# One-column sums moved behind other products, sums copied ahead of tile copies, and the bias table written in eight masked parts

## What is computed

```python
# first block
sh1, sc1, g1, sh2, sc2, g2 = split(silu(c) @ ada_w + ada_b, 6)
h = rms_norm(x) * (1 + sc1) + sh1
x = x + g1 * rms_norm(hybrid_mixer(h))        # 8 heads of attention beside 8 groups of convolution
h = rms_norm(x) * (1 + sc2) + sh2
x = x + g2 * rms_norm(swiglu_ffn(h))
# second block
sh1, sc1, g1, sh2, sc2, g2 = split(silu(c_2) @ w_ada_2 + b_ada_2, 6)
h  = modulate(rms_norm(x), sh1, sc1)
hc = modulate(rms_norm(ctx_2), csh1, csc1)
x = x + g1 * neighbourhood_attention(h, hc)   # scores get a bias from na_rpb_2 and a column mask
x = x + g2 * conv_ffn(modulate(rms_norm(x), sh2, sc2))
```

## Time and profile before

| | us |
|---|---|
| median of 3 runs | 2663.33 (2661.33 to 2666.87) |
| the profiled execution, its own time | 2672.45 |
| its span, first to last instruction | 2670.7 |
| TensorE busy | 2594.7 (97%) |
| VectorE busy | 1839.3 (69%) |
| ScalarE busy | 1301.4 (49%) |
| GpSimd busy | 138.0 (5%) |
| mean share of full TensorE clock granted | 0.986 |

### The profile page before, as it was taken

One profiled execution on the slowest core, in us unless ns is written; L12 is line 12 of the kernel. 1 busy time (PEld: TensorE's weight loads), 2 busy tenths in 40 slices (PEclk: granted clock), 3 DMA queues, 4 the chain that ended last, 5 costly groups with the idle time before them and its releaser, 6 DMA issues.

```text
span 2670.7 us, 38186 instructions
## 1 busy us (share of the span) xinstructions
PE 2594.7 (97%) x13356; PEld 2138.9 (80%) x13356; DVE 1839.3 (69%) x2280; ACT 1301.4 (49%) x1856; POOL 138.0 (5%) x237
## 2 busy tenths in 40 slices
PE   7999899899999999999999999999999999999999
PEld 4677777787788888888787878787888888888887
DVE  2349778777888696888765556555578876667565
ACT  2349655444344344465625242424465556565544
POOL 3112011000200000000001000100000000000000
PEclk8999999899999999999999999999999999999999
DMA  9989777589888687789454545554568866666565
GB/s 352 377 292 370 208 284 247 191 299 335 274 292 284 215 286 254 250 297 324 138 192 142 189 137 177 158 178 142 166 212 283 284 190 190 189 178 203 192 194 167
DMA packets 236447, 622.97 MB, mean 233 GB/s; under 512 B 20172, under 2 KB 24567, under 8 KB 231408
## 3 DMA queue, kind: packets, MB, share of 16 engines
q1 hardware_dynamic: 213392, 525.40, 59.6%
q0 software_dynamic: 22144, 91.84, 10.2%
q10 hardware_dynamic: 800, 4.25, 0.4%
HBM read 613.80 MB, written 7.60 MB: 233 GB/s over the span
## 4 chain that ended last, share of the span: by engine, by line
PE 78%; DMA 10%; DVE 6%; issue 3%; ACT 3%; SPq 0%; DVEq 0%; ACTq 0%; POOL 0%
PE ps L2292 11%; PE ps L2233 11%; PE ps L2237 11%; PE ps L2235 10%; PE ps L2294 6%; PE ps L2687 6%; PE ps L2689 6%; PE ps L2691 6%; DMA raw<-in_w_in 2%; DMA slot<-in_ada_w 2%; DVE w_lo L1393 2%; DMA raw<-in_w_down 2%; DMA ada<-in_ada_w 2%; PE ps L2269 2%; PE ps L2273 1%
## 5 line engine op out<-in xcount | busy, mean ns | idle before, releaser
L1393 DVE TENSOR_TENSOR w_lo<-raw,w_hi 128x1024 fp32r<-128x1024 f32 x762 | 927.2, 1223 | 596.7 <-ACT w_hi L756 594.6
L756 ACT ACTIVATE w_hi<-raw 128x1024 fp32r<-128x1024 f32 x762 | 804.8, 1058 | 1000.3 <-PE ps L2237 406.8
L2292 PE MATMUL ps<-h_both,w_hi 128*128 128x512 f32 (+1 forms) x1392 | 480.7, 392 | 2.7 <-DVE h_both L1471 1.7
L2233 PE MATMUL ps<-w_hi,h_both 128*128 128x512 f32 x1152 | 467.3, 406 | 8.1 <-DVE w_lo L1393 4.8
L2237 PE MATMUL ps<-w_hi,h_both 128*128 128x512 f32 x1152 | 453.4, 394 | 0.0
L2235 PE MATMUL ps<-w_lo,h_both 128*128 128x512 f32 x1152 | 453.0, 393 | 0.0
L2294 PE MATMUL ps<-h_both,w_lo 128*128 128x256 f32 (+1 forms) x1392 | 386.6, 278 | 0.0
L2292 PEld LDWEIGHTS ps<-h_both,w_hi 128*128 128x128 f32 x1392 | 261.2, 188 | 60.9 <-DVE h_both L1471 2.4
L1405 DVE SCALAR_TENSOR_TENSOR acc<-ada,cact,acc 128x1024 f32<-128x1024 f32 x224 | 291.8, 1303 | 8.5 <-DMA ada<-in_w_ada 5.6
L2687 PE MATMUL ps<-w_hi,f_hi 128*128 128x512 f32 x680 | 266.6, 392 | 3.2 <-DVE f_lo L1664 1.8
L2233 PEld LDWEIGHTS ps<-w_hi,h_both 128*128 128x128 f32 x1152 | 218.2, 189 | 60.5 <-DVE w_lo L1393 8.3
(11 more groups left out here) (282 smaller groups left out, 3196.8 us busy)
## 6 DMA issues: line engine op xcount, KB each, us to landing
ada<-in_w_ada SPq DMA_DIRECT2D x192, 512.0 KB, 4.3
raw<-in_ffn_w_up SPq DMA_DIRECT2D x160, 512.0 KB, 4.5
slot<-in_ada_w POOLq DMA_DIRECT2D x60, 1024.0 KB, 9.0
raw<-in_na_w_qkv SPq DMA_DIRECT2D x96, 512.0 KB, 4.8
raw<-in_w_gate SPq DMA_DIRECT2D x88, 512.0 KB, 5.1
raw<-in_w_up SPq DMA_DIRECT2D x88, 512.0 KB, 4.7
raw<-in_w_down SPq DMA_DIRECT2D x88, 512.0 KB, 5.4
raw<-in_ffn_w_down SPq DMA_DIRECT2D x86, 512.0 KB, 4.6
```

Of the source, the lines that this page charges most:

```text
L756: act.activation(w_hi[:, s, :], raw[:, s, :], ACT.Copy).then_inc(hi_ready, 1)
L1393: dve.tensor_tensor(w_lo[:, s, :], raw[:, s, :], w_hi[:, s, :].bitcast(F32), ALU.subtract).then_inc(lo_ready, 1)
L2233: pe.matmul(o, hi_[:, k, a], wh, start=(k == 0), stop=False)
L2292: pe.matmul(ps[:, 4 * part + g, :].rearrange("p (a n) -> p a n", a=2)[:, :, n], w_hi[:, s, a], h_both[:, :, k, n], start=(k == 0 and ts[-1 ...
```

## The change

The diff, cut to its core:

```diff
-        TABLE_DMAS = H2 + 2 * TABLE_PARTS + 1
+        TABLE_DMAS = H2 + 3 * TABLE_PARTS
+        TABLE_AFTER = (4, 18, 32, 46, 56, 62, 68, 74)
...
-            for n in range(TABLE_PARTS):
-                pool.wait_ge(tile_used, T_FF1 + RING + 4 + 7 * n)
+            for n, tile in enumerate(TABLE_AFTER):
+                pool.wait_ge(tile_used, T_FF1 + RING + tile)
+                rows = slice(n * TABLE_ROWS, (n + 1) * TABLE_ROWS)
...
-            v = skew_s[:, :, 0:GRID - W]
-            link(pool.affine_select(out=v, in_=v, compare_op=ALU.is_ge, fill=NEG, base=WH,
-                                    pattern=[[0, H2 * DR], [1, GRID - W]], channel_multiplier=-1))
...
-            pool.dma_start(skew_d, skew_s[:, :, :]).then_inc(table_landed, 16)
+                v = skew_s[:, rows, 0:GRID - W]
+                link(pool.affine_select(out=v, in_=v, compare_op=ALU.is_ge, fill=NEG, base=WH,
+                                        pattern=[[0, TABLE_ROWS], [1, GRID - W]], channel_multiplier=-1))
...
+                pool.dma_start(skew_d[:, rows, :], skew_s[:, rows, :]).then_inc(table_landed, 16)
# ACT, opening
                 if q:
-                    for n in range(6 * q, 6 * q + 3):
-                        hi(T_AG, n)
+                    hi(T_AG, 6 * q)
+                    hi(T_AG, 6 * q + 1)
                 evacuate_sums(2 * q + 1)
                 start_hi(q)
                 if q:
+                    hi(T_AG, 6 * q + 2)
                     hi(T_AG, 6 * q + 3)
# DVE, opening
                 shift_of(2 * q)
-                if q:
-                    lo(T_AG, 6 * q + 2)
                 scale_of(2 * q + 1)
                 start_lo(q)
                 if q:
+                    lo(T_AG, 6 * q + 2)
                     lo(T_AG, 6 * q + 3)
# ACT, between the blocks
+            def b_g1_rows(cs):
+                for c in cs:
+                    act.wait_ge(g1_sums, c + 1)
+                    act.activation(acc0[:, c * C:(c + 1) * C], ps[:, c, :], ACT.Copy).then_inc(g1_read, 1)
...
                     hi(Tend, j)
+                    if j in (5, 6):
+                        b_g1_rows((2 * j - 10, 2 * j - 9))
# DVE, between the blocks
-                after()
...
-            def b_g1_rows():
-                for c in range(4):
-                    dve.wait_ge(g1_sums, c + 1)
-                    dve.tensor_copy(acc0[:, c * C:(c + 1) * C], ps[:, c, :]).then_inc(g1_read, 1)
-                clear(acc1)
...
             for e in range(2, 4):
                 split_ctx(e)
+            dve.wait_ge(g1_sums, 4)
+            clear(acc1)
             dve.wait_ge(acc_bias[1], 64)
# DVE, out_turn
+                y_gated(phase, 0, 0, bufs[1])
                 scale()
-                y_gated(phase, 0, 0, bufs[1])
# PE
-            def column_sums(accs, units_, m_, bank=6):
+            def column_sums(accs, units_, m_, bank=6, after=0):
+                for _ in range(after):
+                    yield
...
-                                             between=between if j > 1 or t == 0 else iter(()))
+                                             between=iter(()) if t else between)
...
-            qkv2(2, 1, between=column_sums((acc1,), 10 * UNITS, M["b_sh2"]))
+            qkv2(2, 1, between=column_sums((acc1,), 10 * UNITS, M["b_sh2"], after=12))
```

More of the change, by code:

```diff
@@ L696, in _ @@
             pool.wait_ge(table_landed, 16 * (H2 + TABLE_PARTS))
-            for n in range(TABLE_PARTS):
-                pool.wait_ge(tile_used, T_FF1 + RING + 4 + 7 * n)
+            W, WH = 16, 8
+            for n, tile in enumerate(TABLE_AFTER):
+                pool.wait_ge(tile_used, T_FF1 + RING + tile)
+                rows = slice(n * TABLE_ROWS, (n + 1) * TABLE_ROWS)
                 src = bass.AP(table_d.tensor, n * TABLE_ROWS * GRID * LANES + GRID - 1,
                               [[LANES - 1, GRID], [GRID * LANES, TABLE_ROWS], [1, GRID]])
-                pool.dma_start(skew_s[:, n * TABLE_ROWS:(n + 1) * TABLE_ROWS, :], src).then_inc(table_landed, 16)
-                pool.wait_ge(table_landed, 16 * (H2 + TABLE_PARTS + n + 1))
-            W, WH = 16, 8
-            v = skew_s[:, :, 0:GRID - W]
-            link(pool.affine_select(out=v, in_=v, compare_op=ALU.is_ge, fill=NEG, base=WH,
-                                    pattern=[[0, H2 * DR], [1, GRID - W]], channel_multiplier=-1))
-            v = skew_s[:, :, W:GRID]
-            link(pool.affine_select(out=v, in_=v, compare_op=ALU.is_gt, fill=NEG, base=WH - W,
-                                    pattern=[[0, H2 * DR], [-1, GRID - W]], channel_multiplier=1))
-            pool.dma_start(skew_d, skew_s[:, :, :]).then_inc(table_landed, 16)
+                pool.dma_start(skew_s[:, rows, :], src).then_inc(table_landed, 16)
+                pool.wait_ge(table_landed, 16 * (H2 + TABLE_PARTS + 2 * n + 1))
+                v = skew_s[:, rows, 0:GRID - W]
+                link(pool.affine_select(out=v, in_=v, compare_op=ALU.is_ge, fill=NEG, base=WH,
+                                        pattern=[[0, TABLE_ROWS], [1, GRID - W]], channel_multiplier=-1))
+                v = skew_s[:, rows, W:GRID]
+                link(pool.affine_select(out=v, in_=v, compare_op=ALU.is_gt, fill=NEG, base=WH - W,
+                                        pattern=[[0, TABLE_ROWS], [-1, GRID - W]], channel_multiplier=1))
+                pool.dma_start(skew_d[:, rows, :], skew_s[:, rows, :]).then_inc(table_landed, 16)
             pool.wait_ge(table_landed, 16 * TABLE_DMAS)
@@ L1803, in out_turn, with down_turn @@
                     lo(Tend, j)
-            def down_turn(n, phase, Tend, bufs, n0, m_, after, beside):
+            def down_turn(n, phase, Tend, bufs, n0, m_, beside):
                 def rows(s_):
@@ L2027, in _ @@
                        True, PH_DOWN1, d_ctx)
-            def b_g1_rows():
-                for c in range(4):
-                    dve.wait_ge(g1_sums, c + 1)
-                    dve.tensor_copy(acc0[:, c * C:(c + 1) * C], ps[:, c, :]).then_inc(g1_read, 1)
-                clear(acc1)
-            down_turn(8, PH_DOWN1, T_QKV2, down_bufs, 18, M["lat"], b_g1_rows, split_ctx)
+            down_turn(8, PH_DOWN1, T_QKV2, down_bufs, 18, M["lat"], split_ctx)
             for e in range(2, 4):
                 split_ctx(e)
+            dve.wait_ge(g1_sums, 4)
+            clear(acc1)
             dve.wait_ge(acc_bias[1], 64)
```

## The result

The changed kernel took 2642.66 us (median of 4 runs, 2637.05 to 2643.56), the kernel before 2662.33 in the same set (4 runs, 2660.57 to 2666.87): ratio 0.9919, 95% interval 0.9900 to 0.9938, 19.7 us less. The forecast was 2637.0 in a range of 2628 to 2652. Two later sets with 5 and 4 runs of the changed kernel gave 25.6 us less (2643.95 against 2669.52, ratio 0.9907, 0.9893 to 0.9922) and 24.5 less (2639.98 against 2664.47, 0.9904, 0.9879 to 0.9928).

The account below looks back on a forecast made before the run. TensorE, busy 2594.7 of 2670.7 us, was taken as the bound, so only its waits and half clock could be won. Terms 4.0 + 9.9 + 4.3 + 1.5 + 6.5 = 26.2 off the median 2663.33 gave 2637.0, range 2628 to 2652.

Parts of the forecast that it names:

- First output product: Sums at the first output product: moved behind the products of `t = 0`, they save wait and half clock, 9.9 us.
- Table: First feed-forward network: eight small masks and writes replace two large masks and one write, removing one TensorE stop, 4.3 us.
- Opening: Opening, fourth quarter: copy to `sums` ahead of ScalarE's third tile, removing TensorE's wait and lost clock, 4.0 us.
- Rival B: Only the sums pay; opening, table and copies between the blocks give nothing: 16.4 us saved, 2646.9; chance 0.14.
- Between the blocks: Between the blocks: ScalarE takes VectorE's four copies ahead of the splits of `ctx_2`, shortening TensorE's wait, 1.5 us.
- Third pass: Sums in the third pass: twelve bare products first (`after=12`) keep the clock full, 6.5 us, bounds 0 to 7.
- Rival A: The clock falls at the sums of first output product and third pass all the same: 11.7 us saved, 2651.6; chance 0.16.
- Rival C: First feed-forward network: each of the table's eight parts makes a stop like the single one, 8.2 us slower, 2671.5; chance 0.03.
- rival D: The change does more than listed: a second `w_lo` wait may go with its clock, 3 us more, 2634; chance 0.05.

Follow-up runs that it names:

- the kernel with `after=0`: Changed kernel with the third pass's sixteen sums directly behind the wait instead of behind twelve products (`after=12`); run twice: 2644.26 and 2638.61 us.

## Why the prediction was right, and where it was off

**First output product** (9.9): measured 8.3 by the medians of one set and 7.4 to 9.2 by profiles; within its bounds of 7 to 12. The mechanism held, including the wait for `w_lo` left at 490.4 and the clock. Of my 9.9, the wait is the smaller part: the profile of the run with the old wait and the new order loses 1.7.

**Table** (4.3): 4.8 by the medians and 4.3 by the profile. I had it all behind the write; in one of three profiles with the old table it came from the mask instead, by the wait of 3.47 us for `acc`. The price of a small mask was too low, mostly 1.2 to 2.3 us for 0.8 beside a working VectorE, and didn't matter.

**Opening** (4.0): 4.0 to 5.8 by 150 us. The fourth quarter gave it, the second little, as argued. Rival B, that the transfers take it back, has the profiles against it: all three with the old opening are 4.0 to 5.8 us later by 150 us, the ten others -2.2 to 0.6. The ratios point the same way. Its price is off too: of its 9.9 + 6.5 for the sums only 8.3 was there.

**Between the blocks** (1.5): 2.3 to 3.9 in profiles, because a short wait there can also drop the clock, which I had left out. The timed runs can't tell it from nothing.

**Third pass** (6.5): the step that failed. It measured 6.5 in one execution of four and nothing in three, and 0.3 and -1.4 in two timed comparisons. I had its bound of 0 for the case that the clock falls anyway after the change; what happened is that it mostly doesn't fall before it either. I should have seen the warning: 2672.45 for the profiled execution against a median of 2663.33 means 9.1 us that most executions don't lose. I read terms from an execution 9.1 us above the median and took them off the median.

Taking the terms as the times give them, 8.3 + 4.8 + (5 to 9) + (-1 to 3) + 0 = 17 to 25, against 19.7, 25.6 and 24.5 in the three sets. So 2637.0 was partly luck: with one of its five terms missing, the sum still comes near because the opening and the copies between the blocks may give more than forecast. That the first set falls 6.5 us short of 26.2, just the missing term, is a coincidence, since the other two sets reach 25.6 and 24.5 without it. Rival A is refuted where it was asked: in none of nine profiles with the new order of the first output product, nor in ten with that of the third pass, is the clock at half for most of the sums. Rival C, a stop for each part, is refuted by 0.3 us of waits for `w_lo` in that network, at most 1.5 in any profile with the new table. For rival D there is a coincidence only: the wait for `w_lo` near 645 us was absent from the second profile of before as well, and from that of the old table.

The rule of the Trainium skill that the prediction weighed ("TensorE: Matmul & The Clock Gate", section "What's actually happening": sustained activity lifts the slow state) can be placed now. Bare products behind a wait of 3.29 us brought the clock back, which agrees. Products alternating with one-column sums, busy for 5.00 of 5.00 us, did not for 13.7 to 17.1 us: busy time as the profile counts it was not enough there.

## What to carry to other kernels

Where TensorE has just been idle for some microseconds, put full products first and narrow ones (one-column sums) behind them: sixteen sums directly behind a wait of 3.4 us, wait included, cost 7 to 9 us here, and the same wait with bare products ahead of the sums 1.7. Behind a wait of 0.94 us the order was worth nothing in the median. Before a stretch at half clock is put down to the order of the code, look at a second profile of the same kernel, and hold the profiled execution's own time against the median: what is above it is bad luck of that one execution, and no change can take it off the median. A large transfer and a large mask that each can stop TensorE once are worth cutting; moving other transfers into a stretch that is already short of them was not.

## What the runs showed of the hardware

The same code, busy throughout and at a granted clock of 1.00, runs at two paces. From about 2150 to 2410 us, in the last feed-forward network, fifty microseconds hold 290 instructions in the first profile of the changed kernel and 285 in that of the kernel with `after=0`:

```profile
2230.00:2280.00 50.00, 50.00 (x290) 43.73 (x289) 31.86 (x38) 28.53 (x33) 0.00 (x0) 1.00 0.61 192
```

```profile
2230.00:2280.00 50.00, 50.00 (x285) 43.32 (x284) 31.75 (x38) 27.84 (x32) 0.00 (x0) 1.00 0.64 187
```

Six of the fourteen profiles have the slower pace there and lose 3.7 to 4.1 us by it, among them the unaltered changed kernel once. None of the edits touches this stretch, nothing in the profile names a cause, and it was not tried. It is one of the reasons that differences under 5 us need several profiles.

GpSimd's masks and VectorE's two-input operations hold each other up. The first mask, begun at 545.13, needs 2.33 us, while two operations of VectorE keep their 1.28 and 1.22: the one that was running and the one that began 0.42 us after the mask. The second mask takes 0.83, and the unit that VectorE began at 547.59 needs 1.91 instead of 1.28. So one of the two keeps its time and the other waits, and the one that starts first doesn't always win (GpSimd, then VectorE):

```profile
545.13 2.33 POOL L707 TENSOR_SCALAR_AFFINE_SELECT skew_s<-skew_s 64x672 f32<-64x672 f32 x1 [3.56 <-DMA skew_s<-rpb_table]
547.60 0.83 POOL L710 TENSOR_SCALAR_AFFINE_SELECT skew_s<-skew_s 64x672 f32<-64x672 f32 x1
```

```profile
544.35 1.28 DVE L1415 SCALAR_TENSOR_TENSOR acc<-ada,cact,acc 128x1024 f32<-128x1024 f32 x1
545.55 1.22 DVE L1403 TENSOR_TENSOR w_lo<-raw,w_hi 128x1024 fp32r<-128x1024 f32 x1
547.59 1.91 DVE L1415 SCALAR_TENSOR_TENSOR acc<-ada,cact,acc 128x1024 f32<-128x1024 f32 x1 [0.83 <-DMA ada<-in_ada_w]
```
